# One transformer block and two hybrid layers in fp32: quartered first loads, four query units in spare buffers, index scores woven into units, and a later place for a job's scores

## The reference, cut to what matters

```
def hybrid_layer(x, norm_g, w_in, ...):
    h = rms_norm(x, norm_g)
    proj = h @ w_in
    q, k, v, gate_a, u_b, gate_b, q_idx, k_idx, w_idx, merge = split(proj)
    q, k = rope(rms_norm(q)), rope(rms_norm(k)); q_idx, k_idx = rope(q_idx), rope(k_idx)
    # indexer, 8 heads of 64: which 128 keys does a query see
    s = einsum('bqhd,bkd->bqhk', q_idx, k_idx)
    score = einsum('bqhk,bqh->bqk', relu(s), w_idx * scale)
    score = where(chunk[key] <= chunk[query], score, NEG)
    sel = top_k(score, 128)
    attn = softmax over sel of (q k) times v          # 8 heads of 64, one k and v for all
    y_a = (attn * silu(gate_a)) @ w_a
    pooled = means of u_b over windows 2, 4, 8, 16 (by group of 128 channels) - u_b
    y_b = ((pooled @ pool_w + pool_b) * pool_s * silu(gate_b)) @ w_b
    g_a, g_b = split(sigmoid(merge))
    return x + (g_a * y_a + g_b * y_b) @ w_out
```

## Time and profile before

| | us |
|---|---|
| median of three runs | 1560.16 |
| the profiled execution | 1556.19 |
| its span, first to last instruction | 1554.3 |
| TensorE busy | 1499.2 (96%) |
| GpSimd busy | 971.3 (62%) |
| VectorE busy | 952.0 (61%) |
| ScalarE busy | 550.9 (35%) |

### The profile page before, as it was taken

How to read it: one execution, slowest core, us unless ns; L and a number is a source line. 1 busy time by engine, 2 the same in 40 slices (tenths; PEclk the granted TensorE clock), 3 DMA queues, 4 the chain that set the end, 5 groups by cost and what they waited for, 6 DMA issues and landing times.

```text
span 1554.3 us, 24339 instructions
## 1 busy us (share of the span) xinstructions
PE 1499.2 (96%) x8516; PEld 1208.8 (78%) x8516; DVE 952.0 (61%) x2033; ACT 550.9 (35%) x1280; POOL 971.3 (62%) x1496
## 2 busy tenths in 40 slices
PE   7999999999999999999999999999998999999999
PEld 7776547678778778877989888889996877777777
DVE  6874781567676640046777788944448789894251
ACT  4446682333333310044564333341125523333100
POOL 6533415656565688776886644546888774455685
PEclk9999999999999999999999999999999999999999
DMA  7210001222222332332222211112222221121223
GB/s 257 66 48 28 28 1 46 77 71 93 93 94 94 94 104 88 96 98 77 89 69 82 69 55 55 55 55 76 95 82 70 87 88 49 48 68 55 68 95 108
DMA packets 37774, 119.42 MB, mean 77 GB/s; under 512 B 5424, under 2 KB 7600, under 8 KB 37424
## 3 DMA queue, kind: packets, MB, share of 16 engines
q1 hardware_dynamic: 36544, 116.06, 23.3%
q10 hardware_dynamic: 1136, 2.09, 0.4%
HBM read 116.02 MB, written 2.10 MB: 76 GB/s over the span
## 4 chain that ended last, share of the span: by engine, by line
PE 79%; DVE 11%; ACT 3%; POOL 3%; issue 3%; DMA 1%; SPq 0%; POOLq 0%; ACTq 0%; DVEq 0%
PE ps L778 62%; PE ps L1240 3%; PE ps L797 2%; PE ps L791 2%; PE ps L980 2%; PE ps L902 2%; POOL wlo L645 2%; PE ps L1315 1%; DVE score L2385 1%; POOL whi L641 1%; DVE score L2384 1%; PE ps L1310 1%; ACT pts L1539 1%; DVE probs L2403 1%; PE ps L1290 1%
## 5 line engine op out<-in xcount | busy, mean ns | idle before, releaser
L778 PE MATMUL ps<-hh,whi 128*128 128x512 f32 (+1 forms) x1448 | 511.4, 353 | 5.3 <-DVE hl L2177 1.7
L778 PE MATMUL ps<-hl,whi 128*128 128x512 f32 (+1 forms) x1448 | 502.8, 347 | 0.0
L778 PE MATMUL ps<-hh,wlo 128*128 128x512 f32 (+1 forms) x1448 | 501.5, 346 | 0.0
L641 POOL TENSOR_SCALAR whi<-raw 128x256 fp32r<-128x256 f32 x564 | 257.8, 485 | 332.9 <-PE ps L778 331.4
L645 POOL TENSOR_TENSOR wlo<-raw,whi 128x256 fp32r<-128x256 f32 x564 | 442.7, 816 | 11.8
L778 PEld LDWEIGHTS ps<-hh,whi 128*128 128x128 f32 x1448 | 273.9, 189 | 59.4 <-issue 11.3
L778 PEld LDWEIGHTS ps<-hh,wlo 128*128 128x128 f32 x1448 | 274.1, 189 | 34.9
L778 PEld LDWEIGHTS ps<-hl,whi 128*128 128x128 f32 x1448 | 274.0, 189 | 33.0 <-issue 0.7
L735 POOL TENSOR_TENSOR wlo<-raw,whi 128x256 fp32r<-128x256 f32 x160 | 134.7, 873 | 92.8 <-ACT whi L1586 92.8
L1959 DVE TENSOR_TENSOR tmp<-tmp 128x512 f32<-128x512 f32 x12 | 10.8, 900 | 118.3 <-ACT tmp L1624 90.0
L778 PE MATMUL ps<-plain_high,whi 128*128 128x264 f32 (+2 forms) x232 | 74.0, 319 | 6.6 <-POOL wlo L645 6.2
(11 more groups left out here) (363 smaller groups left out, 2709.9 us busy)
## 6 DMA issues: line engine op xcount, KB each, us to landing
raw<-in_w SPq DMA_DIRECT2D x197, 512.0 KB, 3.5
raw<-in_w SPq DMA_DIRECT2D x8, 256.0 KB, 3.4
x<-in_x SPq DMA_DIRECT2D x4, 512.0 KB, 8.1
out<-x SPq DMA_DIRECT2D x8, 256.0 KB, 4.4
raw<-in_w SPq DMA_DIRECT2D x12, 128.0 KB, 2.9
raw<-in_w SPq DMA_DIRECT2D x4, 384.0 KB, 3.4
cw_k<-in_cw1k SPq DMA_DIRECT2D x1, 1024.0 KB, 5.5
cw_v<-in_cw1v SPq DMA_DIRECT2D x1, 1024.0 KB, 7.4
```

What stands on the lines that cost most here:

```text
L641: ins = pool.tensor_scalar(whi[s][:, c:c + PIECE], raw[s][:, c:c + PIECE], 1.0, 0.0, ALU.mult, ALU.add)
L778: mm = pe.matmul(out, lhs, rhs, start=start and n == 0, stop=stop and n == 2)
```

## The change

It has five parts.

1. In the head, the value units are loaded in a quarter, a quarter and a half, all quarters first; `wg`, `vec`, x0, x1 (256 KB each) and the next pair are issued on ScalarE's queue. GpSimd, ScalarE and VectorE work on the same pieces, so VectorE has one instruction more before its squares. `spread_root` comes two token blocks earlier.
2. Four of the eight query units of each layer go to spare buffers, two of them in `bh` and `bl`, which are free then. GpSimd's order is written out accordingly.
3. The index scores of a slot are taken out of their place and woven into the slot's last unit: the first pair before it, the others at a quarter, a half and three quarters. ScalarE evaluates their relus and then reads that unit. In two places a unit moves one slot earlier.
4. On TensorE `qk(s + 2)` moves from the slot's start to behind the first turn's transposing product and the first unit.
5. On VectorE `gate_out(s - 1)` and `weighted(s + 1)` come before the masks of job s+2.

```
-        QUERY_EXTRA = [U_LAYER + l * L_UNITS + 2 for l in range(LAYERS)]
+        QUERY_EXTRA = {U_LAYER + l * L_UNITS + 2 + c: spot for l in range(LAYERS)
+                       for c, spot in ((0, 0), (1, 1), (4, 2), (5, 0))}
...
-                units = [..., "ub2", "mg7", "gb3 mg8", "ub3", ...]            # layer 0
+                units = [..., "ub2", "mg7 mg8", "gb3", "ub3", ...]
-                units = ["gb0", "ub0", "mg4", "gb1", "ub1", "mg5", "mg6 gb2", ...]   # layer 1
+                units = ["gb0", "ub0", "mg4", "gb1", "ub1", "mg5 mg6", "gb2", ...]
...
-            sp.dma_start(raw[0][:, 0:HALF], io["w"][FIRST[0]][:, 0:HALF]).then_inc(*tick("half_in0", 0, 16))
-            sp.dma_start(wg[:], io["wg"]).then_inc(*tick("wg_in", 0, 16))
-            sp.dma_start(raw[1][:, 0:HALF], io["w"][FIRST[1]][:, 0:HALF]).then_inc(*tick("half_in1", 1, 16))
-            sp.dma_start(raw_third[:, 0:HALF], io["w"][FIRST[2]][:, 0:HALF]).then_inc(*tick("half_in2", 2, 16))
-            sp.dma_start(vec[:], io["vec"]).then_inc(*tick("vec_in", 0, 16))
-            x_pair(0)
+            sp.dma_start(raw[0][:, 0:PIECE], io["w"][FIRST[0]][:, 0:PIECE]).then_inc(*tick("quarter_in0", 0, 16))
+            sp.dma_start(raw[1][:, 0:PIECE], io["w"][FIRST[1]][:, 0:PIECE]).then_inc(*tick("quarter_in1", 1, 16))
+            sp.dma_start(raw_third[:, 0:PIECE], io["w"][FIRST[2]][:, 0:PIECE]).then_inc(*tick("quarter_in2", 2, 16))
...
+            act.dma_start(wg[:], io["wg"]).then_inc(*tick("wg_in", 0, 16))
+            act.dma_start(vec[:], io["vec"]).then_inc(*tick("vec_in", 0, 16))
+            for k in range(2):
+                act.dma_start(x[:, k, META:T], io["x"][:, k, :]).then_inc(*tick(f"x_one{k}", 0, 16))
+            act.dma_start(x[:, 2:4, META:T], io["x"][:, 2:4, :]).then_inc(*tick("x_in1", 0, 16))
...
@@ GpSimd, each layer
+                split_extra(n)
+                pool.wait_ge(ty.sem("unit_used"), unit_ready(first))
+                split_extra(n + 1)
+                for s in range(2):
+                    split(n // 2 + 1, s, False, unit_ready(first + s))
+                split_extra(n + 4)
+                pool.wait_ge(ty.sem("unit_used"), unit_ready(n))
+                split_extra(n + 5)
...
@@ TensorE, a unit with index scores woven in
+                def lunit(m, out, free=(None, None), half=None, between=()):
+                    if between:
+                        index(*between[0])
...
+                    stops = {i * len(spans) * DC // len(between): between[i] for i in range(1, len(between))}
...
+                            if tok * DC + k in stops:
+                                index(*stops[tok * DC + k])
...
@@ TensorE, a slot
-                    if s + 2 < plan["slots"]:
-                        qk(s + 2)
                     if s:
                         weigh(last_turn[s - 1])
                     spacers = list(plan["units"][s])
+                    indices = [what for kind, what in plan["side"][s] if kind == "index"]
+                    woven = spacers.pop() if indices else None
...
                         if spacers:
                             fill(spacers.pop(0))
-                    for kind, what in plan["side"][s]:
-                        if kind == "index":
-                            index(*what)
+                        if turn == turn0 and s + 2 < plan["slots"]:
+                            qk(s + 2)
                     for f in spacers:
                         fill(f)
+                    if woven:
+                        fill(woven, indices)
...
@@ VectorE, a slot
+                    if s:
+                        gate_out(s - 1)
+                    if s + 1 < plan["slots"]:
+                        weighted(s + 1)
                     if both_banks:
                         for c in mixes:
                             fill(("pm", c))
                     if s + 2 < plan["slots"]:
                         masked(s + 2)
-                    if s:
-                        gate_out(s - 1)
-                    if s + 1 < plan["slots"]:
-                        weighted(s + 1)
                     if s >= 2:
                         low_out(s - 2)
```

More of the change, by code:

```diff
@@ L585, in _ @@
             sp.dma_start(raw_third[:, HALF:DC], io["w"][FIRST[2]][:, HALF:DC]).then_inc(*tick("third_in", 2, 16))
-            for c in range(1, 4):
+            for c in range(2, 4):
                 x_pair(c)
@@ L674, in split_first @@
                 ins.then_inc(ty.sem("unit_high"), 1)
-                pool.wait_ge(ty.sem("unit_high"), p)
+                pool.wait_ge(ty.sem("unit_high"), p + 1)
                 for c in range(0, DC, PIECE):
@@ L705, in third_half @@
                         ins.then_inc(*tick("third_low", c))
-            for half in range(2):
-                first_half(half)
-                third_half(half)
+            for k0, count in ((0, PIECE), (PIECE, PIECE), (HALF, HALF)):
+                first_piece(k0, count)
+                third_piece(k0, count)
             for p in range(3, 16):
@@ L758, in _ @@
             elsewhere += DC
-            for l, n in enumerate(QUERY_EXTRA):
+            for l in range(LAYERS):
+                first = U_LAYER + l * L_UNITS
+                n = first + 2
                 for s in range(2):
-                    split(n // 2 - 1, s, False)
+                    split(first // 2, s, False)
                 if l:
@@ L764, in _ @@
                 split_extra(n)
-                split(n // 2, 1, False)
-                with pool.Fori(n // 2 + 1, (n + L_UNITS) // 2 - 1) as i:
+                pool.wait_ge(ty.sem("unit_used"), unit_ready(first))
[5 more added lines that the diff above has]
+                split_extra(n + 5)
+                for s in range(2):
+                    split(n // 2 + 3, s, False, unit_ready(n + 2 + s))
+                with pool.Fori(n // 2 + 4, (first + L_UNITS) // 2) as i:
                     for s in range(2):
@@ L1130, in weights_of @@
                     return whi[n % 2], wlo[n % 2]
-                def lunit(m, out, free=(None, None), half=None):
+                def lunit(m, out, free=(None, None), half=None, between=()):
+                    if between:
+                        index(*between[0])
                     high, low = weights_of(m)
-                    for tok, (lo, n) in enumerate(cols2(l) if half is None or half[1] != "ub" else [(0, TH), (TH, TH)]):
+                    spans = cols2(l) if half is None or half[1] != "ub" else [(0, TH), (TH, TH)]
+                    stops = {i * len(spans) * DC // len(between): between[i] for i in range(1, len(between))}
+                    for tok, (lo, n) in enumerate(spans):
                         if free[tok]:
@@ L1164, in qunit @@
                         for k in range(DC):
-                            if c == 0:
-                                mm = unit_extra(QUERY_EXTRA[l], out[:, tok, 0:n], k, plain_high[:, k, lo:lo + n],
+                            if place(l, L_QI + c) in QUERY_EXTRA:
+                                mm = unit_extra(place(l, L_QI + c), out[:, tok, 0:n], k, plain_high[:, k, lo:lo + n],
                                                 plain_low[:, k, lo:lo + n])
@@ L1211, in squares_of, with fill @@
                     mm.then_inc(*tick("q_squares", (l, c)))
-                def fill(f):
+                def fill(f, between=()):
                     nonlocal g_free
@@ L1229, in fill @@
                         else:
-                            lunit(unit_of(kind, c), G[:, mine[0]:mine[-1] + 1], [g_free[b] for b in mine], (l, kind, c))
+                            lunit(unit_of(kind, c), G[:, mine[0]:mine[-1] + 1], [g_free[b] for b in mine], (l, kind, c), between)
                         for tok, b in enumerate(mine):
@@ L1893, in _ @@
                         exped2(s + 2)
-                    for kind, what in plan["side"][s]:
-                        if kind == "index":
-                            index(*what)
                     for f in spacers:
                         fill(f)
+                    for what in indices:
+                        index(*what)
+                    if woven:
+                        fill(woven)
                 a_high(plan["slots"] - 2)
@@ L1986, in _, with second_low @@
                 .then_inc(*tick("head_low", ("gate", 1)))
-            def second_low(half):
-                ks = slice(half * HALF, half * HALF + HALF)
-                dve.wait_ge(*at("head_high", ("value", 1, half)))
+            def second_low(k0, count):
+                ks = slice(k0, k0 + count)
+                dve.wait_ge(*at("head_high", ("value", 1, k0)))
                 dve.tensor_tensor(wvl[:, ks, P:2 * P], raw[1][:, ks], wvh[:, ks, P:2 * P].bitcast(F32), ALU.subtract)\
-                    .then_inc(*tick("head_low", ("value", 1, half)))
-            second_low(0)
+                    .then_inc(*tick("head_low", ("value", 1, k0)))
+            second_low(0, PIECE)
             dve.wait_ge(*at("vec_in", 0))
```

70 lines of the change are left out of this document (41 added, 29 removed).

## The result

The changed kernel takes 1598.37 us in the median of four runs (1597.32 to 1600.75), against 1558.14 for the kernel before in the runs beside it: a ratio of 1.0255, 95% interval 1.0234 to 1.0276. That is 40 us slower, outside the forecast's range. The profiled execution has a span of 1595.7 us, 41.4 more than before, with a mean granted clock of 0.977 instead of 0.994.

What follows compares the result with a forecast made beforehand. TensorE was taken as the bound, busy 1499.2 of 1554.3 us. Terms -2.0 - 3.0 - 16.0 + 16.3 + 1.0 = -3.7 us gave a median of 1556.5; own range 1551 to 1562, with rivals 1544 to 1569.

Steps and rivals of the forecast that it cites:

- Parts 4 and 5, forecast +17.3: In both layers' slots: late scores cost 16.3 us, VectorE's new order 1.0 us.
- part 4 alone, forecast +16.3: Slots with pool work: late scores cost 19.6 us over eight slots, of which 16.3 new; ends 0 and 27.
- the carry: Light slots (6.87 us of VectorE) making up for slots with pool work; the forecast took this as lost with late scores.
- a heavy slot costs its excess: Slots with pool work hold 10.59 and 9.90 us of VectorE against TensorE's 7.79: 2.45 us lost each on average.
- the 15 to 20 given as the sign: In the slots: TensorE's waits for VectorE's bank reads rise from some 3 us to 15 to 20 if right.
- The rival on the slower side: Slots: late scores cost more than weaving brings, with 5.8 us of half clock; +7.5, 1567.7 us; chance 0.23.
- Part 1, forecast -2.0: Head: first product up to 3 us earlier, 2.0 counted; GpSimd's next split not earlier; ends 0 and 4.5.
- Part 2, forecast -3.0: Query stretches: GpSimd waits return as one for VectorE; quicker VectorE instructions win 1.5 us a layer; ends 0 and 6.
- the 0 that I had drawn from that page: Query stretches: by the VectorE and GpSimd exclusion rule contention only moves, giving 0 in place of 3.0 us.
- Part 3, forecast -16.0: Index scores: 18.2 us of relu waits go, 8.0 paid for switches, 5.8 won from the clock; ends 8 and 20.
- the 18.2 us "lost waiting for ScalarE's relu": Five bare index blocks: 14.4 of 32.6 us is work by columns, the other 18.2 waits for score banks.
- Part 5, forecast +1.0: Some 20 slots: TensorE meets ScalarE's turned-block copy sooner, 0.05 us each; takes the gate wait off late scores; ends 0 and 4.

Runs made afterwards that it cites:

- part 4 alone: The kernel before with only the scores of job s+2 moved behind the slot's first turned block and unit: 1661.05 us against 1556.18, ratio 1.064.
- parts 3 and 5: The kernel before with woven index scores and VectorE's order mixing step, gate, weigh, masks; scores at the slot's start: 1551.88 us against 1558.39, ratio 0.9962.
- Part 3 alone: The kernel before with only the woven index scores and the two moved units, scores at the slot's start: 1554.31 us against 1558.88, ratio 0.9976.
- part 3 with the wider spread: Woven index scores alone, last two query blocks' selection spread over one slot more, layer 0's last pool unit one slot later: 1560.46 us against 1556.18, ratio 1.0017.
- part 5 alone: The kernel before with VectorE's order mixing step, gate, weigh, masks, the mixing step moved ahead too: 1561.63 us against 1558.39, ratio 1.0026.
- mended: Head change alone on the kernel before, second half of the value unit one pair of rows earlier on ScalarE and VectorE: 1558.96 us against 1558.39, ratio 1.001.

## Why the prediction was wrong, point by point

*Parts 4 and 5, forecast +17.3, are +35 in the changed kernel; part 4 alone, forecast +16.3, is +105 on the kernel before.* This is the step that failed: "Afterwards the carry is gone, and a heavy slot costs its excess: 2.80 and 2.11, mean 2.45." The lateness was seen and the direction was right, the price was not. I priced VectorE's excess of load over one slot, eight times. But VectorE stands at the masks until the scores come, 68.7 us instead of 23.8, with the rest of its queue behind them: part 4 alone brought 66.7 us of idle time to TensorE, where the excess of load is the same 19.6. That the changed kernel's 18.6 us of new idle time lie so near the 17.3 is therefore chance, as the path shows. I named what is queued behind the masks on VectorE and left out ScalarE, whose read of the gate unit waits for VectorE's mixing step and has the turned copies behind it. Of TensorE's waits in the slots 14.1 us end on VectorE, close to the 15 to 20 given as the sign, and 16.7 more on ScalarE, which the forecast did not have; of the six longest, 3.0 to 4.9 us, four end on ScalarE. (The "some 3.3 us" paid before are 2.6: 0.82, 0.96 and 0.82.)

*The clock was a term of nothing in part 4, and priced in a rival only.* The forecast had waits of 2 to 3 us, spread over eight slots, and took 1.00 after them. They came as single waits of 3 to 5 us, each with 3 to 5 us at 0.50 behind it, and this is 15.4 us of the 35. The rival on the slower side had the mechanism, with 5.8 us for it, and its 1567.7 was still 31 us short.

*Part 1, forecast -2.0, is +3.0 in the changed kernel's trace and +3.5 in the median alone.* The first product came at about the time forecast; whether the second queue or the smaller pieces brought it forward, no run separates. The sentence that failed is that GpSimd's next split "is not earlier after the change": it was 3.2 us later, since VectorE's half, on which the reload waits, was moved behind two more instructions. I had the moved instruction in the sum as VectorE's time, and not as a wait of SP's queue.

*Part 2, forecast -3.0, is +6.1 in the two stretches, +4.5 in the median.* That the waits for GpSimd come back as one before the first index score was right, to its place and releaser (9.7 us for L2444). Two terms were wrong. VectorE's rotations did get quicker, by 1.9 and 2.0 us a layer where 1.5 was forecast, but behind the first index score, where nothing waits for them; ahead of it GpSimd worked beside them as long as before and they took 12.7 us for 13.0. And the one long wait costs the clock, 3.4 us a layer. The Trainium skill, "SBUF — State Buffer", Who interferes with whom, has a VectorE instruction with two SBUF inputs and a GpSimd instruction that reads SBUF shut each other out. The trace agrees up to the first index score, where the overlap stayed; the 0 that I had drawn from that page came out for TensorE, and not for VectorE.

*Part 3, forecast -16.0, is -4.6 alone.* The relu waits went and so did both half-speed stretches, as forecast. In the trace 8.7 us are won in layer 0 and 6.5 in layer 1, together near the 16.0; 2.8 of it go at the gate unit's read and 9.8 in the two heavy slots. The terms inside are less good than their sum: the 18.2 us "lost waiting for ScalarE's relu" are block time beyond the columns, of which TensorE was idle for 5.2 and waited 5.0 for relu, and the two stretches were worth 6.8 and not 5.8. That VectorE becomes the limit was priced under part 4 and belongs here too: the faster TensorE reaches VectorE's late work sooner.

*Part 5, forecast +1.0, is -72 with late scores*, and somewhere between +3 and -2 without them (with the mixing step moved too). "It costs VectorE nothing" was right; what it saves, the forecast named and did not price.

## What to carry to other kernels

Before a producer is moved later on one engine, list what stands behind its consumer on the consumer's own queue, and what other engine's queue waits for any of that: the time that the consumer stands is what to look for, and it passes from queue to queue. A handful of waits of 1 to 2 us was cheaper here than one of the same sum; the edit that joined them, part 2, paid some 3 us of half clock in each layer as well. And a part that gains is worth running without its companions: here parts 3 and 5 make 1551.9 us, while all five together make 1598.4.

## What was not expected of the hardware

The first attention, 1050 products whose code and waits are the same in all these kernels (TensorE is idle for 13.9 to 14.6 us of it in each), took anything from 182.2 to 188.0 us. Part 3 alone and part 3 with the wider spread are the same kernel up to there and enter it at 71.36 and 71.46 us; they needed 182.2 and 185.0. Those two ran on two chips; part 5 alone and parts 3 and 5 are alike up to there too, ran on one, and needed 183.1 and 188.0. The difference is TensorE's clock: what the half clock costs in the stage goes from 1.7 to 8.5 us. Ten us from the same product on, before (82 products) and after (58); then the same 951 products, in part 3 alone, and in parts 3 and 5:

```profile
98.00:108.00 10.00, 9.76 (x82) 8.38 (x83) 5.03 (x18) 3.53 (x13) 3.63 (x7) 1.00 0.17 55
```
```profile
101.00:111.00 10.00, 10.00 (x58) 8.57 (x60) 2.40 (x10) 2.71 (x10) 3.64 (x7) 0.66 0.17 54
```
```profile
92.47:253.58 161.11, 148.27 (x951) 95.54 (x950) 95.17 (x403) 94.44 (x312) 44.82 (x81) 0.99 0.07 21
```
```profile
94.02:260.89 166.87, 154.37 (x951) 100.26 (x950) 94.92 (x403) 94.77 (x312) 44.93 (x81) 0.95 0.06 20
```

VectorE and ScalarE did the same work (95 us each). So behind the same short waits the clock falls in one execution and holds in another, and the code does not decide it. One wait of this stage, 1.8 to 1.9 us at the same product in all 16 traces, had half clock behind it in 11 of them and 1.00 in 5. For long waits it was otherwise: all 38 waits of 3.5 us and more in the 16 traces, the one at the kernel's start left out, had half clock behind them.

In the changed kernel this stage is 4.1 of the 41.4 us. Kernels without the new head show the same spread, so these may be chance. But the eight kernels with the new head (mended or not) took 184.5 to 187.8, and of the other eight four took 182.2 to 182.4, so that the head has a part in it is not ruled out.

Single times of one kernel go with the clock too: in one batch the kernel before took 1555.23 us at a mean granted clock of 0.995 and 1565.1 at 0.987. So only a ratio whose interval leaves out 1 is called a difference here, and places are compared by product number and not by the span. A stage's length still carries this chance, some us where the clock fell in it.
